# A hybrid block on one core: the state-space part with the step size folded into x, one masked product for two heads, running sums over 128 rows, and the step-size chain in pieces

## What is computed

```
dt = softplus(dt_raw + dt_bias);  A = -exp(a_log)
y  = ssd_scan(xs * dt, dt * A, B, C) + xs * d_skip        # 32 heads of 64, 4 groups, state 128
y  = y * silu(z);  y = group_rms(y) * norm_w
merged = sigmoid(g_attn) * (a @ w_proj_attn) + sigmoid(g_ssd) * (y @ w_proj_ssd)
x = x + merged @ w_out;   x = x + conv_glu_ffn(rms_norm(x))
```

## Times and profile before

| | us |
|---|---|
| median of 3 executions | 1883.48 |
| lowest, highest | 1883.44, 1883.91 |
| the profiled execution | 1886.26 |
| its span, first to last instruction | 1884.4 |
| PE busy, matmuls (share) | 1783.2 (95%) |
| DVE busy | 1371.4 (73%) |
| ACT busy | 1011.9 (54%) |
| POOL busy | 684.4 (36%) |

### The profile page before, as it was taken

The page is one execution under the profiler, slowest core; times in us unless marked ns, Lnnn a source line. Parts: engine busy times, 40 slices in busy tenths (PEclk is TensorE's granted clock), DMA queues, the critical chain, the costliest instruction groups (busy, mean ns, idle before and its releaser), DMA issues.

```text
span 1884.4 us, 33699 instructions
## 1 busy us (share of the span) xinstructions
PE 1783.2 (95%) x13954; PEld 1711.4 (91%) x13954; DVE 1371.4 (73%) x1981; ACT 1011.9 (54%) x1543; POOL 684.4 (36%) x413
## 2 busy tenths in 40 slices
PE   6989999997999988999999999997999999999998
PEld 5989999886999987998889999996899988999997
DVE  3768765565786747994789589766797488859785
ACT  4465544473654443577564565544376656356562
POOL 5641104561310353344564511036244367341113
PEclk8999999898999989999999999998999999999999
DMA  7335545431455543454234555553355333445542
GB/s 264 135 110 179 205 159 169 157 120 34 158 186 183 179 152 106 157 190 135 90 112 162 173 168 193 174 184 123 112 179 168 112 103 133 167 148 190 202 165 82
DMA packets 80504, 288.28 MB, mean 153 GB/s; under 512 B 8928, under 2 KB 9184, under 8 KB 80224
## 3 DMA queue, kind: packets, MB, share of 16 engines
q1 hardware_dynamic: 79488, 283.15, 44.8%
q10 hardware_dynamic: 864, 2.98, 0.4%
HBM read 285.05 MB, written 1.05 MB: 152 GB/s over the span
## 4 chain that ended last, share of the span: by engine, by line
PE 70%; DVE 22%; ACT 5%; issue 2%; DMA 0%; POOL 0%; ACTq 0%; SPq 0%; DVEq 0%; POOLq 0%
PE lin L637 21%; PE lin L638 21%; PE lin L639 21%; DVE acc L1606 3%; DVE arena L1973 3%; DVE w_lo L452 2%; DVE sq L1964 2%; ACT w_hi L1109 1%; DVE arena L2026 1%; DVE sq L1532 1%; PE stat L926 1%; DVE arena L1867 1%; PE stat L704 1%; PE tr L1025 1%; PE tr L788 1%
## 5 line engine op out<-in xcount | busy, mean ns | idle before, releaser
L637 PE MATMUL lin<-h_hi,w_hi 128*128 128x256 f32 x2976 | 857.6, 288 | 8.6 <-DVE h_lo L461 8.6
L638 PE MATMUL lin<-h_lo,w_hi 128*128 128x256 f32 x2976 | 846.6, 284 | 0.0
L639 PE MATMUL lin<-h_hi,w_lo 128*128 128x256 f32 x2976 | 846.1, 284 | 0.0
L1109 ACT ACTIVATE w_hi<-w_raw 128x1024 fp32r<-128x1024 f32 (+1 forms) x546 | 537.1, 1032 | 387.3 <-PE lin L639 386.1
L452 POOL TENSOR_TENSOR w_lo<-w_raw,w_hi 128x1024 fp32r<-128x1024 f32 (+1 forms) x210 | 506.5, 2422 | 426.6 <-ACT w_hi L1109 420.9
L637 PEld LDWEIGHTS lin<-h_hi,w_hi 128*128 128x128 f32 x2976 | 576.1, 194 | 15.3 <-DVE h_lo L461 8.2
L638 PEld LDWEIGHTS lin<-h_lo,w_hi 128*128 128x128 f32 x2976 | 576.1, 194 | 2.8 <-issue 2.5
L639 PEld LDWEIGHTS lin<-h_hi,w_lo 128*128 128x128 f32 x2976 | 575.7, 193 | 0.0
L452 DVE TENSOR_TENSOR w_lo<-w_raw,w_hi 128x1024 fp32r<-128x1024 f32 (+1 forms) x336 | 475.5, 1419 | 80.7 <-ACT w_hi L1109 75.4
L637 PE MATMUL lin<-hid_hi,w_hi 128*128 128x256 f32 x912 | 260.8, 286 | 2.3 <-DVE hid_lo L461 2.1
L638 PE MATMUL lin<-hid_lo,w_hi 128*128 128x256 f32 x912 | 258.3, 283 | 0.0
(11 more groups left out here) (277 smaller groups left out, 2188.8 us busy)
## 6 DMA issues: line engine op xcount, KB each, us to landing
w_raw<-in_upA SPq DMA_DIRECT2D x112, 512.0 KB, 3.7
w_raw<-in_upB SPq DMA_DIRECT2D x64, 512.0 KB, 4.0
w_raw<-in_xbc SPq DMA_DIRECT2D x48, 512.0 KB, 4.3
w_raw<-in_dnA SPq DMA_DIRECT2D x32, 512.0 KB, 3.6
w_raw<-in_dnB SPq DMA_DIRECT2D x32, 512.0 KB, 3.6
w_raw<-in_z SPq DMA_DIRECT2D x32, 512.0 KB, 4.1
w_raw<-in_gates SPq DMA_DIRECT2D x32, 512.0 KB, 3.8
w_raw<-in_ps SPq DMA_DIRECT2D x32, 512.0 KB, 4.1
```

Source lines behind the costliest of these rows:

```text
L637: nc.tensor.matmul(out, lhs[0], rhs[0], start=first, stop=False)
L638: nc.tensor.matmul(out, lhs[0], rhs[1], start=False, stop=False)
L639: return nc.tensor.matmul(out, lhs[1], rhs[0], start=False, stop=last)
L1109: nc.scalar.activation(w_hi[slab.slot][:, half, part], w_raw[slab.slot][:, half, part], ACT.Copy)\
```

## The change

- **Step size folded into x.** The transposed x is multiplied by dt of its token and head when it is taken out of `stat`, by DVE (`stepped`), in place of ACT's plain copy; DVE issues them between its z work.
- **One masked product for two heads.** `ssd_m` no longer multiplies by dt, so one tensor_tensor of 128x768 does both heads of a c, with `cbm` broadcast over the two. It waits for both exponentials. PE waits once for both heads and does the first token half of both heads, then the second.
- **Running sums.** `cum_hi` and `cum_lo` become rows 0 to 31 and 32 to 63 of one tile `cum_parts` of 128 rows; the rest is zero, filled once at the start. `ident_r` holds the identity twice, the rest zero. One product over 128 rows per head gives hi + lo.
- **Second remainders on DVE.** In the gates stage POOL does half 0 only; DVE does half 1, after each odd c. Two `take_over` waits go. The remainder of the running sum is made by DVE, at xbc slab 1, in place of POOL.
- **Chain in pieces.** |dt| is taken before the rope of ki2. The 16 links are cut into four pieces (5, 3, 3, 5 links), one at the end of each of the four q steps. ACT rounds the running sum at xbc slab 0, behind that slab's roundings, and copies the transposed dt at slab 3; PE transposes dt and the running sum after xbc slab 2.

```diff
+            nc.gpsimd.memset(cum_parts[:, :].bitcast(F32), 0.0)
+            nc.gpsimd.memset(ident_r[:, :].bitcast(F32), 0.0)
@@ POOL, xbc to gates
-                pool.wait_ge(s.cum_hi, l + 1)
-                lo_part(pool, cum_lo[:, :], dtb[0:SH, 2, :], cum_hi[:, :]).then_inc(s.cum_lo, 1)
@@ POOL, gates_weights
-                    split_lo(pool, slab.ahead(SPLIT_AHEAD), 1)
-                take_over(pool, "gates", 1, l)
@@ PE, xbc_slab: dt_by_token() after n == 2, no longer after n == 0
@@ PE, running_sums
-                        head = ident_r[:, 2 * c + i:2 * c + i + 1].to_broadcast([SH, P])
-                        out = logit[:, 2 * (c % 2) + i, :]
-                        nc.tensor.matmul(out, head, cum_hi[:, :], start=True, stop=False)
-                        mm = nc.tensor.matmul(out, head, cum_lo[:, :], start=False, stop=True)
+                        head = ident_r[:, 2 * c + i:2 * c + i + 1].to_broadcast([P, P])
+                        mm = nc.tensor.matmul(logit[:, 2 * (c % 2) + i, :], head, cum_parts[:, :], start=True, stop=True)
@@ PE, y products
+                    pe.wait_ge(s.ssd_m, SH * l + 2 * c + 2)
+                    for t, (to, of) in enumerate(((slice(0, T), slice(0, T)), (slice(P, T), slice(T, T + P)))):
+                        for head in (2 * c, 2 * c + 1):
@@ ACT, xbc_conv
+                    if n == 0:
+                        act.wait_ge(s.dt_chain, DT_LINKS * (l + 1))
+                        nc.scalar.activation(cum_parts[0:SH, :], dtb[0:SH, 2, :], ACT.Copy).then_inc(s.cum_hi, 1)
+                    if n == 3:
+                        act.wait_ge(s.dt_tr, l + 1)
+                        nc.scalar.activation(dt_tok_sb[:, :], tr[:, 0:4 * SH], ACT.Copy).then_inc(s.dt_tok, 1)
@@ ACT, z stage: by_token(2 * u) and by_token(2 * u + 1) go
@@ DVE, before the qi ropes
                 stt(mag, arg, -1.0, arg, ALU.mult, ALU.max).then_inc(s.dt_abs, 1)
-                dve.wait_ge(s.dt_e, l + 1)
+                rope(ki2[:, :, :], 1, "idx")
                 ch = Chain(dve, s.dt_chain, DT_LINKS * l)
-                softplus(ch, dt, arg, None, mag, (adt, cum))
+                def step_sizes(n):
+                    if n == 0:
+                        dve.wait_ge(s.dt_e, l + 1)
+                        softplus_ratio(ch, mag, (adt, cum))
+                    elif n < 3:
+                        softplus_series(ch, (adt, cum), ((13, 11, 9), (7, 5, 3))[n - 1])
+                    else:
+                        softplus_sum(ch, dt, arg, mag, (adt, cum))
+                        dve.wait_ge(s.a_exp, l + 1)
+                        ch.link(ts(adt, dt, small[0:SH, 40:41], -1.0, ALU.mult, ALU.mult))
+                        ch.link(nc.vector.tensor_tensor_scan(cum, adt, adt, 0.0, ALU.add, ALU.min))
@@ DVE, end of each q step
+                    step_sizes(n)
@@ DVE, xbc_taps, after weights(slab)
+                    if n == 1:
+                        dve.wait_ge(s.cum_hi, l + 1)
+                        lo_part(nc.vector, cum_parts[SH:2 * SH, :], cum, cum_parts[0:SH, :]).then_inc(s.cum_lo, 1)
@@ DVE, z stage, behind da_probs and behind the second weights
+                def stepped(b):
+                    t, quarter = XT_ORDER[b]
+                    dve.wait_ge(s.xt_tr, 8 * l + b + 1)
+                    by_head = (P, 8, XI // SH)
+                    out, of = (a.rearrange("p (h n) -> p h n", h=8) for a in (xtok[t][quarter], stat[:, :]))
+                    tt(out, of, dt_tok[:, 0, t, 8 * quarter:8 * quarter + 8].unsqueeze(2).to_broadcast(by_head), ALU.mult)\
+                        .then_inc(s.xt_copied, 1)
@@ DVE, gates stage
+                def ssd_m(c, j):
+                    dve.wait_ge(s.ssd_exp, SH * l + 2 * c + 2)
+                    at = 2 * (j % 2)
+                    tt(m_buf[:, at:at + 2, :], seg_e[:, :, :], cbm.unsqueeze(1).to_broadcast([P, 2, T + P]), ALU.mult)\
+                        .then_inc(s.ssd_m, 2)
                         if j >= 1 or not first:
                             ssd_out(c - 1, j + 3)
+                        if j % 2:
+                            weights(slab_at("gates", c // 2, l))
-                take_over(dve, "pa", 1, l)
```

More of the change, by code:

```diff
@@ L1068, in layer @@
                     bank_read()
[L1069 to L1075 removed]
+                    pe.wait_ge(s.ssd_m, SH * l + 2 * c + 2)
+                    for t, (to, of) in enumerate(((slice(0, T), slice(0, T)), (slice(P, T), slice(T, T + P)))):
+                        for head in (2 * c, 2 * c + 1):
+                            lo = 64 * (head % 2)
+                            by_tok = xtok[t][head // 8][:, head % 8 * 64:head % 8 * 64 + 64]
+                            mm = nc.tensor.matmul(where[lo:lo + 64, to], by_tok, m_buf[:, head % 4, of],
+                                                  start=(t == 0), stop=(t == 1))
                     mm.then_inc(s.ssd_y, 1)
@@ L1357, in _ @@
             act.wait_ge(s.loaded_later, 64)
-            nc.scalar.activation(ident_r[:, :], ident[0:SH, 0:SH], ACT.Copy).then_inc(s.ident_r, 1)
+            for i in range(2):
+                rows = slice(i * SH, (i + 1) * SH)
+                ins = nc.scalar.activation(ident_r[rows, :], ident[rows, rows], ACT.Copy)
+            ins.then_inc(s.ident_r, 1)
             def layer(l):
@@ L1436, in z_silu @@
                         .then_inc(s.bank_free[slab.bank], 1)
-                def by_token(b):
-                    t, quarter = XT_ORDER[b]
-                    act.wait_ge(s.xt_tr, 8 * l + b + 1)
-                    nc.scalar.activation(xtok[t][quarter], stat[:, :], ACT.Copy).then_inc(s.xt_copied, 1)
                 for u in range(4):
@@ L1540, in weights, with softplus, softplus_ratio @@
                     split_lo(dve, slab.ahead(SPLIT_AHEAD), half)
-            def softplus(chain, out, arg, mag, e, scratch):
+            def softplus(chain, out, arg, e, scratch):
+                softplus_ratio(chain, e, scratch)
+                softplus_series(chain, scratch, (13, 11, 9, 7, 5, 3))
+                softplus_sum(chain, out, arg, e, scratch)
+            def softplus_ratio(chain, e, scratch):
                 a, b = scratch
@@ L1549, in softplus, with softplus_series, softplus_sum @@
                 chain.link(ts(b, a, 1.0 / 15.0, None, ALU.mult))
-                for odd in (13, 11, 9, 7, 5, 3):
+            def softplus_series(chain, scratch, odds):
+                a, b = scratch
+                for odd in odds:
                     chain.link(stt(b, b, 1.0 / odd, a, ALU.add, ALU.mult))
+            def softplus_sum(chain, out, arg, e, scratch):
+                a, b = scratch
                 chain.link(stt(b, b, 1.0, e, ALU.add, ALU.mult))
@@ L1739, in _ @@
             dve.wait_ge(s.lam_e, 1)
-            softplus(chain, small[:, 4:8], small[:, 12:16], None, small[:, 8:12], (small[:, 58:62], small[:, 32:36]))
+            softplus(chain, small[:, 4:8], small[:, 12:16], small[:, 8:12], (small[:, 58:62], small[:, 32:36]))
             chain.link(ts(small[:, 0:4], small[:, 4:8], -8.0, None, ALU.mult))
@@ L1835, in rope @@
                     tt(out, out, part, ALU.add).then_inc(s.rope_done, 1)
-                rope(ki2[:, :, :], 1, "idx")
                 dt, adt, cum = (dtb[0:SH, i, :] for i in range(3))
@@ L1953, in layer @@
                         da_probs(u + 1)
+                    stepped(2 * u)
                     weights(slab_at("z", 2 * u + 1, l))
+                    stepped(2 * u + 1)
                 dve.wait_ge(s.dt_tok, l + 1)
```

37 lines of the change are left out of this document (7 added, 30 removed).

## The result

The changed kernel takes 1862.94 us (median of 4 executions, 1862.67 to 1863.91) where the kernel before took 1883.7 beside it: a ratio of 0.9884, with an interval of 0.9872 to 0.9897. The forecast was 1860, with 1854 to 1866 as its own range. By the ratio that is 21.8 us saved. The profiled execution of after took 1862.73 (span 1860.9), so 23.5 us less than that of before (1886.26); the sum of the prediction was 23.6. Two of the terms in it were wrong by more than 5 us over the two layers, with opposite signs, so the total says little about the reasons.

The account below looks back on a forecast made before the run. PE was taken to bound the kernel (busy 1783.2 of 1884.4 us), DVE close behind. 2x(6.8+4.8)+0.4 = 23.6 us off the profiled 1886.26 gave 1862.7; less 2.8 for the median, 1860, own range 1854 to 1866.

Parts of the forecast that it names:

- The front: q stage: chain in pieces removes PE's 7.2 us rope wait and 1.8 us at half clock, 9.0 us a layer.
- The 1.2 us for the last swap and da_logits: Last q steps: swap and da_logits(0) wait for a rope because DVE runs later, 1.2 us a layer lost.
- another 1.0 us: xbc: PE waits for the tightest slab's second remainder because DVE is late, 1.0 us a layer lost.
- The second rival: Late chain: pieces meet POOL's splits, xbc gives back 6 not 2.2 us a layer; 1867.5 us, chance 0.12.
- The gates, 4.8 us: Gates stage: four c's take 18.7 instead of 20.07 us, saving 4.8 us a layer; bounds 0 and 11.
- PE's own 17.3: Gates: PE work per four c's, 20.07 less 1.3 of present waits and 1.5 saved, 17.3 us.
- the sum's 20.07: Gates before the change: length taken for every two slabs and four column blocks c, 20.07 us.
- The first rival (flat gates): Gates: PE's saving becomes only more waiting for the late mask, 20.07 stays; 1869.5 us, chance 0.20.
- the third (PE at the pace): Gates: PE sets the pace at 17.3 us per four c's, 11 us a layer saved; 1847.5 us, chance 0.12.
- z, 0.4 in layer 0 only: Start of z: one ACT copy less brings the second transposes 0.4 us earlier in layer 0.
- The tail and fills: Merged tail: bn's 0.7 us wait may move to h_lo; two POOL fills lie in idling: nothing, uncovered 0.6.

Follow-up runs that it names:

- e5: Kernel before with only the softplus chain in pieces, remainder of the running sum staying on POOL: 1868.35 us, ratio 0.9906.
- e1: Changed kernel with the remainder of the running sum made at xbc slab 6 instead of slab 1: 1851.72 us, ratio 0.9822.
- e8: Changed kernel with the masked product as one 128x384 op per head, each behind its own exponential: 1855.76 us, ratio 0.9841.
- e7: Changed kernel with the single running-sum product per head over 64 rows, not padded to 128: 1865.39 us, ratio 0.9886.
- e4: Changed kernel with both remainders of the gates stage made by POOL again: 1863.72 us, ratio 0.9885.
- e6: Kernel before with only the running sums over 128 rows, one product per head: 1884.58 us, ratio 0.9995.
- e11: Changed kernel with the running-sum remainder at xbc slab 6 and one masked-product op per head: 1846.11 us, ratio 0.9786.
- e10: Changed kernel with the eight token copies back on ACT, multiplication by the step size left out: 1866.56 us, ratio 0.99.
- e9: Changed kernel with running sums as before, two products per head over 32 rows, new mask kept: 1869.42 us, ratio 0.9911.

## Why the prediction was right in sum, and where not

The number was right in part by luck: 23.6 against 23.5 us holds for one pair of profiled executions, and the terms below miss by 8.0 us on one side and 7.5 on the other.

**The front, 9.0 us: right.** Measured 8.75 and 9.15. The swap is at 717.10 (forecast 717.3) with no wait and both of its records at full clock. Timeline of PE in after, beside the earlier trace rows:

```profile
717.10 1.02 PE L923 MATMUL stat<-sq,cst 128*128 128x512 f32 x2
717.56 0.68 PE L634 MATMUL lin<-h_hi,w_hi 128*128 128x256 f32 x1
```

The rope ahead of it stands behind a POOL split, as was allowed for, and is done by 715.13:

```profile
712.95 2.18 DVE L1843 TENSOR_TENSOR arena<-arena,sq 128x512 f32<-128x512 f32 x1
```

**The 1.2 us for the last swap and da_logits: half.** The swaps lost nothing (50.45 in every kernel with the pieces), da_logits 0.6 (e5).

**The failed step: "another 1.0 us" of xbc.** This is the term that failed: it measured 6.0 and 4.9 us (e1 against after). The step went as follows: slack 1.3 us of the tightest slab, DVE 2.4 late from the pieces, plus the remainder of the running sums ("0.42 free, up to 2.5 behind a split"), less what PE lost. The slab was the right one. Counted from the last swap, its w_lo is done at 26.9 us in before (790.13 less 763.25), at 27.6 in e1 (781.75 less 754.17) and at 32.3 in after (786.67 less 754.36). So the pieces make DVE 0.7 late (e5 has the same 27.6) and not 2.4, and the remainder 4.7 and not at most 2.5: 2.7 for its own stall, and 2.0 for the second stall that its lateness brings, which the sum did not look for. That the pieces cost so little has to do with stalls too: between the last swap and this w_lo four DVE ops of before stand behind a split, for 6.6 us over what the same forms take elsewhere, and in e5 such ops stand for some 1.2. The sum took the contention of before over as it was. PE wants it at 28.8 in after (half a slab behind 780.27): 3.5 us of waiting. And behind the wait come 2.3 us lost at 1.2 GHz: the front's sum had counted such a stretch as a gain (1.8), xbc's sum had none as a loss. The second rival had the size ("xbc gives back 6") but put it on the pieces; e5 shows that they give back 0.6.

**The gates, 4.8 us: too small, 7.4 measured.** The forecast had 18.7 us per four c's; measured are 17.85, 17.99 and 18.47 in layer 0 (18.83 in layer 1), and PE's own 17.3 was 17.0 (e8). The mask waits were put at 1.4 per four c's and are 1.1 (8.8 over eight stretches). Before, the three stretches are 19.25, 20.08 and 20.09, so the sum's 20.07 was high for the first, and they gain 5.1 us where the sum has 4.1 for three. The start of the stage gains 0.4, and all from the fourth group on 1.8, where the sum had 0.8 after taking 0.6 away for the last c. That PE saves 6.0 a layer was right (5.9), and so was the part of the changed shape in it (2.4 by e7), but 4.0 of it came out as waiting. The forecast took the shorter block (a single split in place of a pair) for a part of the gain; e4 shows none from it while one op does both heads.
The first rival (flat gates) holds for the sums alone (e6) and not for the change; the third (PE at the pace) describes e8 and e11.

**z, 0.4 in layer 0 only: too small.** 0.75 and 1.76; of these 0.6 a layer are the copies (e10), 0.2 the sums (e9), and 1.0 in layer 1 is the half clock that did not come back.

**The tail and fills: right.** The wait for h_lo is 8.6 before and after, that of bn goes from 1.1 to 0.7 over both layers. The fills are not to be told from the movement of the first stage's start (704.05 and 703.91).

**From the profile to the median: 2.9 us off.** The sum gave 1862.7 for the profiled execution, which took 1862.73. I then took 2.8 off, since the profile of before lay that far above its median. That of after lies 0.2 below its own. The offset was the luck of one execution and should not have been carried over; the medians of before in the later rounds are 1885.34 to 1886.75, so it was rather the median of three executions that lay low.

Per layer 0 and 1 the errors were, in us of time saved against the sum: q -0.3 and +0.2, xbc -4.4 and -3.3, gates +2.6 each, z +0.35 and +1.8. They add to -0.5.

## What to carry to other kernels

An op put on a busy engine costs what its lateness does to the ops behind it: shift the engine's next ops by the delay, lay them beside the next two or three ops of the engine that can block it, and look for a second collision before taking the excess over the slack; or put the op where its result is still far from being used, which here was worth 11 us. Work taken off an engine is worth something only when that engine sets the stage's pace, so try the edits in pairs: the halved running sums brought 0.3 us a layer alone and 1.9 behind the new mask. And count a wait of PE of several microseconds together with the half-clock stretch behind it, on the loss side as on the gain side.

## What the runs showed of the hardware that was not expected

- L1879, a DVE op with a single input tile of 128x256, took 1.21 us in after, ending 0.15 behind a POOL split, and 0.34 in before, where no split lay beside it. So not only two-input ops stand. The Trainium skill (SBUF — State Buffer, Who interferes with whom) names tensor_scalar among the ops that can take the shared ports; this row agrees.

```profile
771.92 1.21 DVE L1879 TENSOR_SCALAR arena<-arena,small 128x256 f32<-128x256 f32 x1
```

- The granted clock was 0.50 for 5.3 us behind a PE wait of 3.4 us in after. Behind one of 1.7 us at the start of z it stayed at 1.00 in layer 0 of before and was 0.50 in layer 1 of the same execution.
- Running sums over 32 rows follow each other at 0.12 us (e9, below), as full products do; a change of shape is seen at its borders, 0.23 instead of 0.12. Over 64 rows (e7) and 128 (after) the stage is as long within 0.15 us, but PE is busy for 77.08 and 74.68 us of it: from the first of two running sums to the slab behind them it is 0.43 us over 64 rows and 0.34 over 128.

```profile
906.68 0.38 PE L1038 MATMUL logit<-cum_parts,ident_r 32*128 32x256 f32 x1
906.91 0.28 PE L1039 MATMUL logit<-cum_lo,ident_r 32*128 32x256 f32 x1
907.02 0.28 PE L1038 MATMUL logit<-cum_parts,ident_r 32*128 32x256 f32 x1
```

- One DVE op of 128x768 took 0.96 us, two of 128x384 took 1.21 (below, e11): the second op costs 0.25 us, and is worth it where the first half can start 0.66 us earlier.

```profile
916.83 1.21 DVE L2002 TENSOR_TENSOR arena<-sq,arena 128x384 f32<-128x384 f32 x2
```
